# A pair table laid out by slot row, output products ahead of the last attention transposes, and a last tile summed on two engines

## The chip, the cores and the metric

The kernel runs on one core of one Trainium2 chip. The metric is the device time of one execution in microseconds (us). Besides its engines (TensorE or PE for matmuls, VectorE or DVE, ScalarE or ACT, GpSimd or POOL, SyncE or SP for queueing transfers) the core has 16 DMA engines, which all queues share.

## What is computed

One layer of an encoder over a prompt of 256 tokens and a sample of 512, in float32, model width 1024. Both sequences use the same weights and attend only within themselves.

```python
h = _rmsnorm(x, attn_norm[l])
proj = h @ w_in[l]
a = _mla(c_q, c_kv, k_pe, ...)              # 8 heads, latent attention
b = _diff_attention(dq, dk, dv, ...)        # 4 heads, (softmax1 - lam * softmax2) @ v, rmsnorm per head
x = x + jnp.concatenate([a, b], axis=-1) @ w_out[l]
x = x + _hier_moe(_rmsnorm(x, ffn_norm[l]), ...)
return _rmsnorm(x, final_norm)

# _hier_moe: the best of 4 groups, in it the best 2 of 8 experts
out = out + gates[:, e:e + 1] * ((silu(t @ w_gate[e]) * (t @ w_up[e])) @ w_down[e])
```

## The kernel before

The 768 tokens are 6 tiles of 128 (NT = 6; tiles 0 and 1 are the prompt). The order of each engine's work is written out by hand, engine by engine, and semaphores tie the engines together. An engine takes its instructions in that order, so one that waits holds back all that stand behind it. The stages:

**Attention.** 48 units (a head pair or a diff head, for one tile of queries) go through a pipeline on TensorE: score, `transpose_p` two steps later, `attend` three steps later. When the last unit of a batch of diff heads is through, ScalarE takes the outputs from the bank, GpSimd computes the norm of the batch (`od_norm`, L480 to L487) and scales it (`od_scale`, L729), TensorE transposes it (`transpose_o`, L1673), and VectorE copies it to `aT` (L1268). Behind the last unit `out_part(0, ...)` (L1690), the output projection of tile 0, is woven in. `out_part(t, part)` does the products `part` of the 16 of tile t (8 for each half of the columns; each is two matmuls in the trace).

**Output projection and routing.** For t = 1 to 5 TensorE does the 16 products of tile t, and among them, for tile t - 1, `x2_transpose` (L1721), `router` (L1732), whose result the semaphore `logits` tells to VectorE, and `rank` (L1745 to L1749), which counts with the masks of `route` which row of its expert's list a token gets. VectorE does for each tile: `residual` halves (L1283), copy of the transposes (L1289), `ffn_norm` (L1299), `route` (L1309 to L1328, a chain of small operations in which each waits for the last; L1323 and L1328 make the two masks), `place` and `slots` (L1361, L1365). TensorE waits for `ones_ready` ahead of tile 1's products: VectorE sets the ones (L1277) behind its last work on the attention.

**The pair table.** `pair_of_slot` in DRAM has 12 x 64 x 32 entries: block, slot row, expert. It is filled with a mark at the start (L536), GpSimd scatters the pair numbers of each tile into it (L745), two for each tile, the last two when all tiles are routed, and SyncE then loads all but block 0 of it twice, for the two halves of the partitions (L613). VectorE waits for both (`ids_further`, L1412 to L1414), between its work for expert 0 and that for expert 1. Block 0 comes from a product (`ids_main`) and needs no table.

**Experts.** TensorE runs each expert on up to 64 rows, and again for further blocks of a popular one: gate and up products (L1806, 32 matmuls), transposes of the next expert's rows (L1797), down products of the expert before (L1815), a transpose of h (L1845). ScalarE does silu (L1060), VectorE the product with up (L1436) and copies (L1441, L1457). Weights come through a ring of six slots.

**The end.** The two expert rows of each pair are loaded (L629, L631). For tiles 0, 2 and 4 VectorE adds them to the residual, times their gates (L1483, L1486); for tiles 1, 3 and 5 TensorE does it with diagonal matrices in two banks (L1915). `total_row(t)` is the sum in either place. ScalarE squares and takes the root (L1113, L1114), VectorE scales (L1491, L1493), SyncE stores. In VectorE's order: combine(4), final(2), final(3), final(4), final(5).

Two lines that the change turns on:

```python
ids_dram.rearrange("(b r e) o -> r b (e o)", b=NBLK, e=NE)      # L536, L614: 32 entries at a time
dve.scalar_tensor_tensor(slot_u[:, 2 * t:2 * t + 2], rank_f, float(NE), slot_f, ALU.mult, ALU.add)  # L1365
```

## Time and profile before

| | |
|---|---|
| median of 3 runs | 780.86 us (780.75 to 782.1) |
| profiled execution | 780.85 us |
| its span, first to last instruction | 779.1 us |
| mean granted TensorE clock | 0.987 |
| busy: TensorE / VectorE / ScalarE / GpSimd | 737.5 / 297.1 / 220.3 / 201.2 us |
| attention's last transposes | 375.3 us |
| output projection and routing | 359.7 to 480 us |
| experts | 481.5 to 747.3 us |
| last pair rows landed / last store issued | 769.7 / 776.9 us |

A row of a timeline has the start, the duration, the engine and line, the operation, what it writes and reads, how many instructions are merged, and in brackets the idle time of its engine before it and what ended that. The granted clock of TensorE is a share of its full 2.4 GHz; it has a second level of one half.

### The profile page before, as it was taken

To read this page: it belongs to the slowest core of one execution; us is meant where nothing else is said; L and a number is where in the kernel's file an instruction comes from. 1 tells how busy PE (TensorE), PEld (TensorE's weight loads), DVE (VectorE), ACT (ScalarE), POOL (GpSimd) and SP (SyncE) were. 2 spreads that over 40 slices of the span, in tenths; PEclk is the share of its full clock that TensorE was granted. 3 is DMA by queue.
4 is the path that set the end of the run, shared out by engine and by line. 5 is a ranking of instruction groups with operands and counts; after the bars stand their busy time and mean duration, and the time that the engine had idled before them with its cause. 6 is when DMAs were issued, how large, how long until landed. Compare 5 with 4: busy or idle time off the path is not lost.

```text
span 779.1 us, 12116 instructions
## 1 busy us (share of the span) xinstructions
PE 737.5 (95%) x3886; PEld 408.2 (52%) x3887; DVE 297.1 (38%) x812; ACT 220.3 (28%) x595; POOL 201.2 (26%) x474
## 2 busy tenths in 40 slices
PE   8999999999888999998999998899997999999995
PEld 4555554444355666665455565455553555555542
DVE  2442211010188989983445455112111121112127
ACT  3643211101176777663111121011111011111123
POOL 1232422220024220330201133253342434342110
PEclk9999999999999999999999998999999999999999
DMA  9703003000140000000598427999999779999748
GB/s 345 277 0 109 0 1 108 1 0 1 42 181 1 2 1 1 2 1 1 201 424 321 163 83 259 377 413 415 415 416 416 268 275 409 419 415 406 275 155 345
DMA packets 36887, 154.64 MB, mean 198 GB/s; under 512 B 9652, under 2 KB 10804, under 8 KB 23904
## 3 DMA queue, kind: packets, MB, share of 16 engines
q1 hardware_dynamic: 28112, 136.50, 44.6%
q0 software_dynamic: 7504, 15.23, 5.3%
q10 hardware_dynamic: 1216, 2.23, 0.8%
q8 instruction: 28, 0.46, 0.3%
q14 instruction: 27, 0.22, 0.1%
HBM read 142.29 MB, written 20.03 MB: 208 GB/s over the span
## 4 chain that ended last, share of the span: by engine, by line
PE 82%; DMA 7%; issue 3%; POOL 3%; DVE 2%; ACT 2%; SPq 1%; POOLq 0%; DVEq 0%; ACTq 0%
PE banks L1534 20%; PE banks L1806 17%; PE banks L1690 9%; PE banks L1815 9%; PE banks L1606 4%; PE banks L1641 4%; PE banks L1797 3%; PE banks L1660 2%; PE banks L1615 2%; PE banks L1557 2%; DMA arena<-pair_rows 2%; PE banks L1664 2%; DMA arena<-h_rows,arena 2%; PE banks L1570 1%; PE banks L1560 1%
## 5 line engine op out<-in xcount | busy, mean ns | idle before, releaser
L1534 PE MATMUL banks<-arena 128*128 128x512 f32 (+1 forms) x384 | 162.1, 575 | 2.0 <-issue 1.6
L1806 PE MATMUL banks<-arena 128*64 128x256 f32 x1280 | 148.8, 385 | 2.8 <-DVE arena L1457 0.9
L1806 PEld LDWEIGHTS banks<-arena 128*64 128x64 f32 x1280 | 93.6, 138 | 50.8 <-issue 6.6
L1534 PEld LDWEIGHTS banks<-arena 128*128 128x128 f32 x384 | 71.5, 191 | 78.3 <-issue 78.3
L1690 PE MATMUL banks<-arena 128*128 128x512 f32 x192 | 86.4, 598 | 1.1 <-DVE arena L1277 1.1
L1815 PE MATMUL banks<-arena 128*64 128x512 f32 x320 | 79.8, 610 | 1.2 <-ACT arena L1068 0.9
L1232 DVE TENSOR_REDUCE arena<-banks 128x1 f32<-128x512 f32 (+1 forms) x96 | 55.4, 599 | 48.8 <-PE banks L1606 42.0
L989 ACT ACTIVATE arena<-banks,arena 128x512 f32<-128x512 f32 (+1 forms) x96 | 58.4, 614 | 43.2 <-DVE arena L1235 22.2
L1436 DVE TENSOR_TENSOR arena<-arena,banks 128x128 f32<-128x128 f32 x40 | 11.6, 290 | 151.3 <-ACT arena L1060 151.2
L1690 PEld LDWEIGHTS banks<-arena 128*128 128x128 f32 x192 | 35.1, 190 | 38.8 <-issue 37.5
L1060 ACT ACTIVATE arena<-banks 128x128 f32<-128x128 f32 x40 | 11.2, 279 | 153.6 <-PE banks L1806 153.6
L769 POOL DMA_INDIRECT arena<-h_rows,arena x40 | 41.8, 1045 | 44.2 <-POOL arena L774 28.7
L918 ACT ACTIVATE arena<-banks,arena 128x512 f32<-128x512 f32 (+1 forms) x24 | 16.0, 667 | 104.7 <-PE banks L1534 104.7
L782 POOL DMA_INDIRECT pair_rows<-arena x36 | 36.4, 1012 | 31.5 <-POOL arena L780 31.5
L1641 PE MATMUL banks<-arena 128*128 128x128 f32 x240 | 36.2, 282 | 8.5 <-issue 5.2
L1641 PEld LDWEIGHTS banks<-arena 128*128 128x128 f32 x240 | 25.9, 141 | 31.0 <-issue 26.0
L1606 PE MATMUL banks<-arena 96*128 96x512 f32 (+1 forms) x96 | 40.0, 539 | 2.1 <-ACT arena L989 1.2
L480 POOL TENSOR_SCALAR arena<-arena 128x2 f32<-128x2 f32 (+1 forms) x8 | 1.6, 195 | 151.9 <-ACT arena L1017 151.9
L1068 ACT ACTIVATE arena<-banks 128x512 f32<-128x512 f32 x32 | 19.1, 597 | 70.1 <-PE banks L1815 70.1
L658 POOL TENSOR_TENSOR arena<-arena 128x64 f32<-128x64 f32 (+2 forms) x24 | 8.0, 333 | 115.9 <-ACT arena L918 67.5
L1815 PEld LDWEIGHTS banks<-arena 128*64 128x64 f32 x320 | 20.1, 137 | 27.4 <-issue 23.7
L1212 DVE COPY arena<-banks 128x512 f32<-128x512 f32 x12 | 8.3, 689 | 64.2 <-PE banks L1580 64.2
(204 smaller groups left out, 900.1 us busy)
## 6 DMA issues: line engine op xcount, KB each, us to landing
arena<-w_gate SPq DMA_DIRECT2D x32, 1024.0 KB, 11.3
arena<-w_up SPq DMA_DIRECT2D x32, 1024.0 KB, 11.1
arena<-w_down SPq DMA_DIRECT2D x32, 1024.0 KB, 11.2
arena<-w_in SPq DMA_DIRECT2D x3, 2048.0 KB, 8.2
arena<-pair_rows SPq DMA_DIRECT2D x5, 1024.0 KB, 11.2
arena<-w_out SPq DMA_DIRECT2D x1, 4096.0 KB, 13.0
arena<-x SPq DMA_DIRECT2D x6, 512.0 KB, 10.2
residual<-arena SPq DMA_DIRECT2D x6, 512.0 KB, 7.1
```

What stands on the lines that cost most here:

```text
L769: pool.indirect_dma_start(x_rows[i], None, h2_dram, bass.IndirectOffsetOnAxis(ap=rows, axis=0), bounds_check=2 * T - 1, oob_is_err=False). ...
L782: pool.indirect_dma_start(y_dram, bass.IndirectOffsetOnAxis(ap=yid_cur[:, i:i + 1], axis=0), y_sb[i], None, bounds_check=4 * T - 1, oob_is ...
L989: act.activation(p_tok[u % 3][:, a, 0:nt * P], bank(2 * (u % 2) + a)[:, 0:nt * P], ACT.Exp, bias=nbias[:, u % 4, a:a + 1], scale=MLA_SCALE ...
L1068: act.activation(y_sb[s % YBUF], bank(4), ACT.Copy).then_inc(y_out, 1)
L1232: dve.reduce_max(mx[:, u % 4, a:a + 1], bank(2 * (u % 2) + a)[:, 0:nt * P], X_).then_inc(dve_chain, 1)
L1534: last = nc.tensor.matmul(bank(mm % 2)[:, 0:GROUP_COLS[g]], xgT[:, t, c, :], w[:, c, :], start=(c == 0), stop=(c == DC - 1))
L1606: nc.tensor.matmul(bank(2 * (u % 2) + a)[:, 0:nt * P], qT[0:QK, 2 * j + a, tok], kT[0:QK, 2 * j + a, keys], start=True, stop=True).then_in ...
L1641: last = nc.tensor.transpose(bank(4 + tau % 2)[:, kt * P:(kt + 1) * P], p_tok[u % 3][:, a, kt * P:(kt + 1) * P], ident)
L1690: last = nc.tensor.matmul(bank(2 * (t % 2) + h), aT[:, t, c, :], w_out_sb[:, c, h * 512:(h + 1) * 512], start=(c == 0), stop=(c == DC - 1))
L1797: last = nc.tensor.transpose(bank(b)[:, c * P:(c + 1) * P], x_rows[i][:, c * P:(c + 1) * P], ident)
L1806: last = nc.tensor.matmul(bank(b)[h * SLOTS:(h + 1) * SLOTS, 0:2 * P].rearrange("p (g n) -> p g n", g=2), x_eT[i][:, 2 * (c % 4) + c // 4, ...
L1815: last = nc.tensor.matmul(bank(4)[h * SLOTS:(h + 1) * SLOTS, :], h_T[:, j * SLOTS:(j + 1) * SLOTS], w[:, j, h * 512:(h + 1) * 512], start= ...
```

## The change

It has three parts.

The pair table is laid out slot row first, then block, then expert: a pair of rank r with its expert e goes to (r mod 64) x 384 + (r div 64) x 32 + e, in place of r x 32 + e. The fill and the two loads then take each slot row in one piece. VectorE gets three operations more in `slots`.

On TensorE the first 8 products of tile 0 go ahead of `transpose_p` of the last unit (their wait for the exponentials is for the unit before it), four products of tile 1 go ahead of the last `transpose_o`, and the rest of tile 1's products is dealt out anew: 6, transposes, 3, router, rank, 3. Tiles 2 to 5 keep 3, transposes, 3, router, 7, rank, 3.

The last tile's sum is split: VectorE makes columns 0 to 511 (`combine_last`, ahead of final(4)), TensorE columns 512 to 1023. ScalarE squares the halves one by one, VectorE's first, and joins them through the bias of the root.

```diff
 
+        def total_half(t, h):
+
+            half = slice(h * 512, (h + 1) * 512)
+            return x_fin[:, t, half] if t == NT - 1 and h == 0 else total_row(t)[:, half]
+
         class Area:
...
         rank_f = m.take(2)
+        rank_u = m.take(2).bitcast(u32)
+        assert 1 << 6 == SLOTS
         onehot = m.take(2 * P).rearrange("p (i n) -> p i n", i=2)
...
             sp.wait_ge(consts_set, 2)
-            sp.dma_start(ids_dram.rearrange("(b r e) o -> r b (e o)", b=NBLK, e=NE),
-                         yids_sb[0:SLOTS, :].rearrange("r (b e) -> r b e", b=NBLK)).then_inc(ids_zeroed, 16)
+            sp.dma_start(ids_dram.rearrange("(r n) o -> r (n o)", r=SLOTS), yids_sb[0:SLOTS, :]).then_inc(ids_zeroed, 16)
             sp.wait_ge(odT_ready, 8)
...
             for h in range(2):
-                sp.dma_start(yids_sb[h * SLOTS:(h + 1) * SLOTS, NE:].rearrange("r (b e) -> r b e", e=NE),
-                             ids_dram.rearrange("(b r e) o -> r b (e o)", b=NBLK, e=NE)[:, 1:, :]).then_inc(ids_loaded, 16)
+                sp.dma_start(yids_sb[h * SLOTS:(h + 1) * SLOTS, NE:],
+                             ids_dram.rearrange("(r n) o -> r (n o)", r=SLOTS)[:, NE:]).then_inc(ids_loaded, 16)
             with sp.Fori(1, NGRP - 1) as g:
...
             act.wait_ge(act_chain, chain[0])
-            for t in range(NT):
+            for t in range(NT - 1):
                 if on_pe(t):
                     act.wait_ge(summed, t // 2 + 1)
                 else:
                     act.wait_ge(y_added, t // 2 + 1)
                 link(act.activation(junk_e, total_row(t), ACT.Square, accum_out=ss[:, t:t + 1]))
                 act.activation(rs[:, t:t + 1], ss[:, t:t + 1], ACT.Sqrt, bias=const("eps"), scale=1.0 / D).then_inc(rms_ready, 1)
+            for h, what, count in ((0, y_added, NT // 2 + 1), (1, summed, NT // 2)):
+                act.wait_ge(what, count)
+                link(act.activation(junk_e[:, h * 512:(h + 1) * 512], total_half(NT - 1, h), ACT.Square, accum_out=ss_c[:, h:h + 1]))
+                if h == 0:
+                    link(act.activation(ss_c[:, 0:1], ss_c[:, 0:1], ACT.Identity, bias=const("eps"), scale=1.0 / D))
+            act.activation(rs[:, NT - 1:NT], ss_c[:, 1:2], ACT.Sqrt, bias=ss_c[:, 0:1], scale=1.0 / D).then_inc(rms_ready, 1)
 
...
                 dve.wait_ge(dve_chain, chain[0])
-                dve.scalar_tensor_tensor(slot_u[:, 2 * t:2 * t + 2], rank_f, float(NE), slot_f, ALU.mult,
+                link(dve.tensor_copy(rank_u, rank_f))
+                link(dve.tensor_scalar(rank_u, rank_u, 6, None, ALU.logical_shift_right))
+                link(dve.scalar_tensor_tensor(slot_f, rank_u, float(NE - SLOTS * NBLK * NE), slot_f, ALU.mult, ALU.add))
+                dve.scalar_tensor_tensor(slot_u[:, 2 * t:2 * t + 2], rank_f, float(NBLK * NE), slot_f, ALU.mult,
                                          ALU.add).then_inc(slots_ready, 1)
...
                 link(dve.reciprocal(rs[:, t:t + 1], rs[:, t:t + 1]))
-                for half in ([slice(0, D)] if t < NT - 1 else [slice(0, 512), slice(512, D)]):
-                    dve.scalar_tensor_tensor(y_rows[:, 2 * t, half], total_row(t)[:, half], rs[:, t:t + 1], gain_fin[:, half],
+                if t < NT - 1:
+                    dve.scalar_tensor_tensor(y_rows[:, 2 * t, :], total_row(t), rs[:, t:t + 1], gain_fin,
                                              ALU.mult, ALU.mult).then_inc(final_ready, 1)
+                    return
+                for h in range(2):
+                    half = slice(h * 512, (h + 1) * 512)
+                    if h == 0:
+                        dve.wait_ge(summed, NT // 2)
+                    dve.scalar_tensor_tensor(y_rows[:, 2 * t, half], total_half(t, h), rs[:, t:t + 1], gain_fin[:, half],
+                                             ALU.mult, ALU.mult).then_inc(final_ready, 1)
+
+            def combine_last():
+
+                t = NT - 1
+                dve.wait_ge(yrows_in[t], 16)
+                x = x_fin[:, t, 0:512]
+                link(dve.scalar_tensor_tensor(x, y_rows[:, 2 * t, 0:512], gates[:, 2 * t:2 * t + 1], x, ALU.mult, ALU.add))
+                dve.scalar_tensor_tensor(x, y_rows[:, 2 * t + 1, 0:512], gates[:, 2 * t + 1:2 * t + 2], x, ALU.mult,
+                                         ALU.add).then_inc(y_added, 1)
 
...
                 final(t - 1 if t else 0)
+            combine_last()
             final(NT - 2)
...
                         pe.wait_ge(o_mla, len([u for u in range(N_UNITS) if is_mla(u) and UNITS[u][0] == 0]))
+                        pe.wait_ge(exps, 2 * N_UNITS - 2)
+                    if t == 1 and i == 0:
                         pe.wait_ge(exps, 2 * N_UNITS)
...
                     score(i)
+                if i == N_UNITS + 1:
+                    out_part(0, range(0, DC))
                 if 0 <= i - 2 < N_UNITS:
                     transpose_p(i - 2)
                 if 0 <= i - 3 < N_UNITS:
                     attend(i - 3)
                 u = i - O_LAG
-                if 0 <= u < N_UNITS and ends_batch(u):
+                if 0 <= u < N_UNITS - 1 and ends_batch(u):
                     transpose_o(u)
 
-                if i in (N_UNITS + 1, N_UNITS + 3):
-                    half = (i - N_UNITS) // 2
-                    out_part(0, range(half * DC, (half + 1) * DC))
+                if i == N_UNITS + 3:
+                    out_part(0, range(DC, 2 * DC))
 
...
 
+            out_part(1, range(0, 4))
+            transpose_o(N_UNITS - 1)
             pe.wait_ge(ones_ready, 1)
             for t in range(1, NT):
-                out_part(t, range(0, 3))
+                out_part(t, range(0, 3) if t > 1 else range(4, 10))
                 if t >= 2:
                     place(t - 2)
                 x2_transpose(t - 1, 0)
                 x2_transpose(t - 1, 1)
-                out_part(t, range(3, 6))
+                out_part(t, range(3, 6) if t > 1 else range(10, 13))
                 router(t - 1, 0)
                 router(t - 1, 1)
-                out_part(t, range(6, 13))
+                if t > 1:
+                    out_part(t, range(6, 13))
                 rank(t - 1)
...
                 last = None
-                for h in range(2):
+                for h in range(2) if t < NT - 1 else (1,):
                     half = slice(h * 512, (h + 1) * 512)
```

TensorE around the end of the attention, before. L1641 is `transpose_p`, L1660 and L1664 are `attend`, L1690 `out_part`, L1673 `transpose_o`, L1721 `x2_transpose`, L1732 `router`, L1747 the first product of `rank(0)`:

```order
L1641 MATMUL banks<-arena 128x128 x4
L1660 MATMUL banks<-arena 64x128 x8
L1690 MATMUL banks<-arena 128x512 x8
L1664 MATMUL banks<-arena 128x128 x4
L1690 MATMUL banks<-arena 128x512 x8
L1673 MATMUL banks<-arena 128x128 x4
L1690 MATMUL banks<-arena 128x512 x3
L1721 MATMUL banks<-arena 128x128 x8
L1690 MATMUL banks<-arena 128x512 x3
L1732 MATMUL banks<-arena 128x36 x8
L1690 MATMUL banks<-arena 128x512 x7
L1747 MATMUL banks<-arena 128x32
```

And now, with L1673 for `transpose_p`, L1692 and L1696 for `attend`, L1724 for `out_part`, L1705 for `transpose_o`, L1756, L1767, L1782 and L1784 for the transposes, the router and both products of the rank:

```order
L1724 MATMUL banks<-arena 128x512 x8
L1673 MATMUL banks<-arena 128x128 x4
L1692 MATMUL banks<-arena 64x128 x8
L1696 MATMUL banks<-arena 128x128 x4
L1724 MATMUL banks<-arena 128x512 x12
L1705 MATMUL banks<-arena 128x128 x4
L1724 MATMUL banks<-arena 128x512 x6
L1756 MATMUL banks<-arena 128x128 x8
L1724 MATMUL banks<-arena 128x512 x3
L1767 MATMUL banks<-arena 128x36 x8
L1782 MATMUL banks<-arena 128x32
L1784 MATMUL banks<-arena 128x32
```

The 8 products went ahead of the last `transpose_p`, four (the last of the 12) ahead of `transpose_o`, and the 7 that stood between router and rank of tile 0 are gone from there.

VectorE at the end of the program, before (scaling of tiles 2, 3, 4 and 5; L1491 is the reciprocal ahead of each):

```order
L1493 SCALAR_TENSOR_TENSOR arena<-arena 128x1024
L1491 RECIPROCAL arena<-arena 128x1
L1493 SCALAR_TENSOR_TENSOR arena<-banks,arena 128x1024
L1491 RECIPROCAL arena<-arena 128x1
L1493 SCALAR_TENSOR_TENSOR arena<-arena 128x1024
L1491 RECIPROCAL arena<-arena 128x1
L1493 SCALAR_TENSOR_TENSOR arena<-banks,arena 128x512 x2
```

And now, from the scaling of tile 3 on:

```order
L1506 RECIPROCAL arena<-arena 128x1
L1508 SCALAR_TENSOR_TENSOR arena<-banks,arena 128x1024
L1523 SCALAR_TENSOR_TENSOR arena<-arena 128x512
L1524 SCALAR_TENSOR_TENSOR arena<-arena 128x512
L1506 RECIPROCAL arena<-arena 128x1
L1508 SCALAR_TENSOR_TENSOR arena<-arena 128x1024
L1506 RECIPROCAL arena<-arena 128x1
L1515 SCALAR_TENSOR_TENSOR arena<-arena 128x512
L1515 SCALAR_TENSOR_TENSOR arena<-banks,arena 128x512
```

Two operations of 512 columns, the last tile's first half, stand between the scalings of tiles 3 and 4.

ScalarE at the end, before (square and root of tiles 4 and 5, behind the root of tile 3):

```order
L1114 ACTIVATE arena<-arena 128x1
L1113 ACTIVATE arena<-arena 128x1024
L1114 ACTIVATE arena<-arena 128x1
L1113 ACTIVATE arena<-banks 128x1024
L1114 ACTIVATE arena<-arena 128x1
```

And now (square and root of tile 4, then the last tile):

```order
L1119 ACTIVATE arena<-arena 128x1024
L1120 ACTIVATE arena<-arena 128x1
L1123 ACTIVATE arena<-arena 128x512
L1125 ACTIVATE arena<-arena 128x1
L1123 ACTIVATE arena<-banks 128x512
L1126 ACTIVATE arena<-arena 128x1
```

One square and one root of the last tile became square, scaled sum, square, root.

## Rows read from the trace of the kernel before

**Rows 1.** The chain that ended last, its share of the span by engine (page):

```profile
PE 82%; DMA 7%; issue 3%; POOL 3%; DVE 2%; ACT 2%; SPq 1%; POOLq 0%; DVEq 0%; ACTq 0%
```

**Rows 2.** Timeline of all engines from 340 to 396 us, TensorE's rows:

```profile
375.35 0.65 PE L1673 MATMUL banks<-arena 128*128 128x128 f32 x4 [0.74 <-POOL arena L729]
...
377.11 2.84 PE L1690 MATMUL banks<-arena 128*128 128x512 f32 x6 [1.10 <-DVE arena L1277]
```

**Rows 3.** The chain in order of time, 345 to 396 us: start, us, what:

```profile
385.11 6.09 PE banks L1690 x14
391.20 0.14 PE banks L1747 x2
```

**Rows 4.** Timeline of VectorE from 376 to 440 us:

```profile
385.15 0.26 DVE L1309 SCALAR_TENSOR_TENSOR arena<-banks,arena 128x36 f32<-128x36 f32 x1 [1.14 <-PE banks L1732]
...
387.31 0.24 DVE L1323 TENSOR_SCALAR arena<-arena 128x32 f32<-128x32 f32 x1
...
388.54 0.24 DVE L1328 TENSOR_SCALAR arena<-arena 128x32 f32<-128x32 f32 x1
...
392.69 0.16 DVE L1365 SCALAR_TENSOR_TENSOR arena<-arena 128x2 uint32<-128x2 f32 x1
394.33 0.69 DVE L1283 TENSOR_TENSOR arena<-arena,banks 128x512 f32<-128x512 f32 x1 [1.48 <-PE banks L1690]
```

**Rows 5.** Stretches (us, busy, PEclk, DMA share, GB/s), then TensorE's timeline:

```profile
496.00:500.00 4.00, 3.65 (x22) 0.62 1.05 408
...
606.00:608.00 2.00, 2.00 (x10) 0.50 0.58 234
...
496.35 4.97 PE L1806 MATMUL banks<-arena 128*64 128x256 f32 x32 [0.49 <-DVE arena L1457]
...
503.97 3.67 PE L1806 MATMUL banks<-arena 128*64 128x256 f32 x32
...
595.49 0.63 PE L1797 MATMUL banks<-arena 128*128 128x128 f32 x4 [2.63 <-DMA arena<-h_rows,arena]
...
604.38 0.67 PE L1797 MATMUL banks<-arena 128*128 128x128 f32 x4 [2.68 <-DMA arena<-h_rows,arena]
```

**Rows 6.** The table load: SyncE, landing, stretches, then timelines of VectorE and TensorE:

```profile
487.55 1.33 SPq L613 DMA_DIRECT2D arena<-pair_of_slot x2
...
DMA to landing us min/median/max: 3.9/4.8/5.7
...
490.00:491.00 1.00, 1.00 1.04 208
...
493.00:494.00 1.00, 1.00 1.02 418
...
493.89 0.34 DVE L1412 TENSOR_SCALAR arena<-arena 128x352 uint32<-128x352 uint32 x1 [7.18 <-DMA arena<-pair_of_slot]
...
495.13 0.29 DVE L1436 TENSOR_TENSOR arena<-arena,banks 128x128 f32<-128x128 f32 x1
...
490.85 1.94 PE L1815 MATMUL banks<-arena 128*64 128x512 f32 x8
495.47 0.39 PE L1845 MATMUL banks<-arena 128*128 128x128 f32 x1 [2.68 <-DVE arena L1436]
```

**Rows 7.** Timelines from 738 us on; the last two rows are ScalarE's at 465 us:

```profile
769.74 3.70 PE L1915 MATMUL banks<-arena 128*128 128x512 f32 x8 [1.76 <-DMA arena<-pair_rows]
...
772.26 1.28 DVE L1493 SCALAR_TENSOR_TENSOR arena<-arena 128x1024 f32<-128x1024 f32 x1
...
773.48 1.12 ACT arena L1113 x2
...
775.15 1.41 DVE L1493 SCALAR_TENSOR_TENSOR arena<-banks,arena 128x512 f32<-128x512 f32 x2
...
465.09 0.62 ACT L1024 ACTIVATE arena<-arena 128x512 bf16<-128x512 f32 x1
...
465.84 0.29 ACT L1030 ACTIVATE arena<-arena 128x1 f32<-128x1 f32 x1
```

## The prediction

> **What bounds the kernel now.** I read the chain of waits first: TensorE carries 82% of it [rows 1], so an edit counts where it moves TensorE or where TensorE stands still. Then I read the timelines of the three stretches that the edit touches, engine by engine. The reader is to see three things. (a) Behind the attention TensorE stands 0.74 us until GpSimd has scaled the last batch, and 1.10 us until VectorE has set the ones [rows 2]; after that it works without a gap through the routing stage, and VectorE's routing chains run beside products [rows 3, 4]. (b) At 492.8 us TensorE has nothing to do for 2.68 us, since VectorE waits for the pair table, and the products behind it run at the lower clock [rows 5, 6]. (c) Behind the last pair rows, TensorE, ScalarE and VectorE follow each other one at a time [rows 7]. The sum is made against the profiled execution: 780.85 us, of which 779.1 is its span; the median of the runs is 780.86, so the same sum serves both.
>
> **Part 1, the pair table by slot row.** Removed: each of the two loads of the table (L613) takes 64 x 11 pieces of 128 bytes; they become 64 pieces of 1408 bytes. The first load is issued at 487.55 and lands 3.9 us later, at 491.5; the second lands at 493.87, where VectorE goes on, 5.7 us behind an issue at 488.2 [rows 6]. So the second comes in 2.4 us behind the first though it was issued 0.65 behind it, and while they run the queues move 208 GB/s instead of the 418 just behind them [rows 6]: the small pieces cost time of their own. With an eleventh of the pieces both should land between where the first landed (491.5) and a point not long after their issue. What follows the landing on VectorE: three operations on the table, from 493.89 to 495.13, 1.24 us, then the product of silu and up (0.29, L1436). TensorE's down products end at 490.85 + 1.94 = 492.79 [rows 6]. It is not held at all if the h product ends by then: landing at or before 492.79 - 0.29 - 1.24 = 491.26. I take that (the upper end, 491.5, is only 0.24 later), so the 2.68 us of idle time go, and with them the short wait for VectorE's copy behind it. Only the transpose of h (L1845, 0.33) stands between the down products and the next gate and up products, so the group that starts at 496.35 starts near 493.1: 3.25 us earlier. That group also took 4.97 us against 3.67 for the same 32 matmuls one expert later, since the granted clock was 0.62 in 496 to 500 [rows 5]; without the gap it should be at full clock: 1.3 us more. Part 1 gains 3.25 + 1.3 = 4.55, say 4.6; bounds: 0 (landing set by the weight loads ahead of it in the queue alone) to 4.7. I take 4.6, since 208 GB/s is a row on exactly these pieces.
>
> The Trainium skill ("DMA: Bandwidth & Descriptors", section "Anatomy of one DMA", written for GpSimd's path) speaks against this part: a transfer costs a fixed 2 us, mostly the receipt of the last write, plus its bytes, and many descriptors can be issued before their number shows. By it the two loads of 88 KB cost about 2.2 us in either layout, the rest of 5.7 us is queueing behind the weights, and part 1 gains next to nothing; the row of 208 GB/s disagrees.
>
> Added to part 1: three chained VectorE operations of two columns in each of the six slots steps. The nearest row is L1365, 0.16 us, and with the hand-over 0.2, so 0.6 us per tile. For five tiles the next thing on VectorE is the second residual half, which stood 1.48 us waiting for TensorE [rows 4]: covered, and 0.6 us dearer each if that cover were gone. For the last tile the scatter is issued from GpSimd several us later than the slots are there. The clearing store at the start is one issue long ahead of its use. These cost nothing. Scatter addresses change, their number and size do not: nothing.
>
> **Part 2, output products ahead of the last transposes.** Moved first: the 8 products of tile 0, first half, go from behind the last unit's transposes and the products of the unit before it to ahead of them. TensorE had no gap between those, and the last attend came behind all of it anyway; its transposed input is copied by VectorE beside the other unit's attend. Nothing gained, and nothing lost as long as that copy is no longer than that attend. Moved second: four products of tile 1 go ahead of the transposes of the last batch (L1673). They cover the 0.74 us wait for GpSimd [rows 2]: -0.7. The wait for the ones (1.10) stays where it was, right behind these transposes, because VectorE sets them only after it has read the transposes: 0. Who waits behind: SyncE's loads of gain, bias and weights start with VectorE's copy of these transposes, now some 2.7 us later; of these tile 0's norm needs the gain and the bias, and that norm too moves back, by the same and by three products more, so it is covered. The weights are wanted a whole stage later.
>
> Moved third, and dearest: tile 1 had 7 products between router(0) and rank(0). They took 6.09 us of the stretch from 385.11 [rows 3] and hid VectorE's route(0). In the new order all of tile 1's products but the last three are spent before the router, and the rank products stand directly behind it. They need the masks of L1323 and L1328. Those are made from 385.15 on and are there at 387.31 + 0.24 = 387.55 and at 388.54 + 0.24 = 388.78 [rows 4]. So TensorE has to stand from router end for 3.7 us (385.11 to 388.82), less the 0.14 us of the first two rank matmuls: 3.55. A restart behind a gap costs some 0.25 more (six matmuls took 2.84 behind the gap at 377.11, where 14 in a row took 6.09, 0.435 each: 2.61) [rows 2, 3]. Part 2 in work and idle time: -0.7 + 3.55 + 0.25 = +3.1. Nothing hides it: the chain runs through TensorE from here to the end of routing.
>
> Then the clock. TensorE stood 2.68 us before 495.5 and before 604.4, and both times it worked at the lower of its levels behind it (0.62 over four us; the products behind the first took 4.97 instead of 3.67) [rows 5]. It stood 2.63 us before 595.5, and did not fall. The new gap is 3.7 us with two matmuls of 32 columns in it, longer than all of these. I take the fall: 1.3 to 1.4 us, the price paid at 496. Part 2: +4.5; bounds 2.9 (no fall) to 5.0.
>
> **Part 3, the last tile's sum.** The rows land at 769.7. Before, TensorE makes both halves in 3.70 us from 769.74, ScalarE squares 1024 columns from 773.48 (1.12) and takes the root (0.3 as in L1030), VectorE scales twice (775.15 on) [rows 7]. Now VectorE makes the first half, but it is busy with tiles 2 and 3 until 772.1 (its scaling of tile 4 starts at 772.26, behind a reciprocal). Two operations on 512 columns at 0.7 each, the half of 1.41 for two of that size: done at 773.5, just when TensorE used to be done. ScalarE then does, one behind the other: square of 512 columns (0.75, from 465.09 to 465.84), the scaled half sum (0.3, L1030), square of the other half (0.75), root (0.3): 2.1 instead of 1.42 [rows 7]. TensorE's half is ready at 771.6 and waits. So the last reciprocal comes 0.65 us later. Tile 4's own output also goes behind by 1.45 us and shares the queues with the last two halves: 0 to 0.3. Part 3: +0.8; bounds 0.6 to 1.2; it loses unless ScalarE took the finished half first, and the order written takes the late one first.
>
> **The sum.** -4.6 + 4.5 + 0.8 = +0.7; with 780.86 that is 781.6. I say 781.5.
>
> **Rivals.**
> 1. The table load gains next to nothing, because the weight loads ahead of it on the same queue set its landing. VectorE still waits until about 493.5, the gap and the low clock stay. (This is also what comes out by the Trainium skill's page above.) For: the queues are full, 418 GB/s behind it. Against: the 2.4 us between two landings [rows 6]. It ends on the slower side: -0.4 + 4.5 + 0.8 = +4.9, 785.8; a half measure (landing at 492.5, TensorE held 1.2 us) would be 783. It decides if the landing is after 492.8. Chance 0.15.
> 2. The clock holds through the new gap, because the two rank matmuls stand in it. For: the gap before 595.5. Against: the gaps before 495.5 and 604.4, both shorter. 781.5 - 1.4 = 780.1. Chance 0.18.
> 3. The clock falls at some other gap that it now survives: the gap before 595.5 is as long as the two that fell, and both parts shift where the gaps lie. +1.4: 782.9. Chance 0.14.
> 4. The stall behind router(0) isn't there, because the masks come sooner than TensorE (route(0) hidden by something I don't see): -4.6 - 0.7 + 0.8 = -4.5, 776.4. Against: the order of both engines is written out, and each step of route(0) waits for the one before. Chance 0.10, with smaller gains elsewhere that I miss.
> 5. My forecast: 0.43.
>
> **Numbers.** A measurement of this kernel tells 0.2% (1.6 us) from no change: the bounds are 779.3 and 782.4. The forecast and rival 2 lie inside, rivals 1 and 3 mostly above, rival 4 below. Faster 0.12, same 0.55, slower 0.33. The range reaches to rival 3 and the half measure of rival 1 above, and to rival 2 with part 3 at its lower end below: 778.9 to 784.3.
>
> **What would show it.** Part 1: the gap of VectorE before its first table operation falls from 7.18 us to under 4.5, TensorE has no gap near 493, and the group of 32 matmuls there takes 3.7 instead of 5.0. Part 2: no wait for GpSimd before the transposes of the last batch, and a wait of about 2.4 and one of 1.1 us before the first and the second pair of rank matmuls of tile 0, with a granted clock under 1 behind them. Part 3: ScalarE's square of the last tile starts with VectorE's half at about 0 to 0.1 us after the time at which TensorE's both halves were done, measured from the landing of the last rows, and the last scaling ends 0.7 us later than before on that scale. The prediction is wrong if the table lands after the down products end, or if rank(0) doesn't wait.

## The result and the profile after

| | before | changed |
|---|---|---|
| median, 8 runs each on one chip | 781.97 us (780.75 to 784.84) | 787.4 us (785.18 to 789.3) |
| profiled execution | 780.85 us | 787.19 us |
| its span | 779.1 us | 785.3 us |
| mean granted TensorE clock | 0.987 | 0.977 |

The change costs 0.70% (95% interval of the ratio 1.0047 to 1.0093), 5.4 us by the medians. 781.5 us had been forecast, with a range of 778.9 to 784.3, so the result lies above the range, and near rival 1 (785.8, +4.9).

I cut the two profiled spans at marks that both programs have: the start of the last attention matmuls, TensorE's first product of `place(0)`, its first gate product and the end of the experts' last gate and up products (the last down products and the summing stand behind that mark). "Low" is the time lost to the lower clock in that stage, worked out from the granted clock of windows of 1 us: TensorE's busy time in each, times what the clock lacks to 1.

| stage | before, us (low) | changed, us (low) | difference |
|---|---|---|---|
| up to the last attention matmuls | 356.4 (1.7) | 358.4 (4.8) | +2.0 |
| to `place(0)`: the moved products, `router(0)`, `rank(0)` | 40.3 (0.0) | 45.8 (3.0) | +5.5 |
| to the first gate product | 84.9 (3.4) | 84.9 (3.2) | 0.0 |
| experts, to the last gate and up products | 261.3 (3.2) | 259.1 (3.4) | -2.2 |
| from there to the end | 36.3 (0.0) | 37.1 (0.0) | +0.8 |

The chain of waits reads as before [rows 1], TensorE carries it (shares by engine in the changed kernel's page):

```profile
PE 83%; DMA 7%; DVE 3%; issue 3%; POOL 2%; ACT 1%; SPq 0%; POOLq 0%; ACTq 0%; DVEq 0%
```

The first row of the table isn't the change's work: both programs do the same there, but the clock stood lower. These are windows of before (first) and of the changed kernel (stretch, its length, busy time of TensorE, of its weight loads, VectorE, ScalarE and GpSimd, then PEclk, DMA share, GB/s). They lose 0.06 x 26.3 = 1.6 us and 0.17 x 27.2 = 4.6 us. In the profiles of this study that place loses anything from 0 to 5.1 us, with the same TensorE instructions in all of them:

```profile
200.00:230.00 30.00, 26.27 (x119) 14.56 (x117) 15.56 (x53) 14.17 (x53) 1.93 (x10) 0.94 0.39 144
```

```profile
200.00:230.00 30.00, 27.23 (x108) 15.65 (x107) 13.23 (x45) 11.97 (x44) 0.39 (x3) 0.83 0.37 144
```

The other rows are the three parts. **Part 2** first: TensorE's timeline of the changed kernel (start, duration, line, what was merged, idle time ahead), beside which [rows 2, 3] stand for before, then its windows:

```profile
379.90 0.60 PE L1705 MATMUL banks<-arena 128*128 128x128 f32 x4
381.60 5.42 PE L1724 MATMUL banks<-arena 128*128 128x512 f32 x12 [1.10 <-DVE arena L1289]
...
390.31 1.87 PE L1767 MATMUL banks<-arena 128*128 128x36 f32 x16
394.76 0.61 PE L1782 MATMUL banks<-arena 128*128 128x32 f32 x2 [2.58 <-DVE arena L1335]
395.90 0.63 PE L1784 MATMUL banks<-arena 128*128 128x32 f32 x2 [0.53 <-DVE arena L1340]
```

```profile
392.00:396.00 4.00, 0.89 (x5) 0.67 (x4) 3.26 (x16) 0.00 (x0) 0.00 (x0) 0.83 1.01 404
396.00:400.00 4.00, 4.00 (x7) 1.93 (x8) 2.92 (x20) 0.72 (x2) 0.00 (x0) 0.50 1.01 425
400.00:404.00 4.00, 4.00 (x9) 1.72 (x8) 0.69 (x1) 1.31 (x4) 0.00 (x0) 0.81 1.02 426
```

The wait for GpSimd ahead of `transpose_o` (L1705) is gone, the one for the ones (1.10) is the same as in [rows 2], and `rank(0)` stands for its two masks, 2.58 and 0.53 us. Just ahead of the first of its matmuls the clock falls, and it comes back only behind 401 us: 0.17 x 4 + 0.5 x 4 + 0.19 x 4 = 3.4 us of clock, of which 3.0 while TensorE worked.

The kernel before has such a place itself, and I had overlooked it: `rank(5)`, the last one, with four products between router and rank instead of seven, waits for the same two masks (L1747 and L1749 are `rank`'s products with them). TensorE's timeline of before, then its windows:

```profile
470.34 0.41 PE L1747 MATMUL banks<-arena 128*128 128x32 f32 x2 [0.95 <-DVE arena L1323]
471.57 0.53 PE L1749 MATMUL banks<-arena 128*128 128x32 f32 x2 [0.82 <-DVE arena L1328]
```

```profile
472.00:476.00 4.00, 4.00 (x14) 2.97 (x14) 2.43 (x18) 0.00 (x0) 0.00 (x0) 0.50 0.74 300
476.00:480.00 4.00, 3.97 (x8) 1.35 (x6) 1.63 (x8) 0.00 (x0) 2.56 (x3) 0.68 0.16 43
```

Behind two waits of under 1 us the clock is low from 471 to 479 us and TensorE loses 3.3 us of work. That is the row nearest to the new stall, on the same instructions, and its price is what the new stall cost. It isn't the same in every profile: behind the same two waits t_first_old and t_first_new (below) hold the upper level.

**Part 1**: the table load in the changed kernel. SyncE's timeline first, to be read beside [rows 6]:

```profile
487.00 1.29 SPq L554 DMA_DIRECT2D arena<-w_down  x3
494.92 1.13 SPq L619 DMA_DIRECT2D arena<-pair_of_slot  x2
497.10 0.35 SPq L554 DMA_DIRECT2D arena<-w_gate  x1
```

The answer on line 619, and the windows (stretch, length, PEclk, DMA share, GB/s):

```profile
DMA to landing us min/median/max: 3.2/4.1/5.0
```

```profile
497.00:498.00 1.00, 1.00 0.68 213
498.00:499.00 1.00, 1.00 0.95 223
```

VectorE's and then TensorE's timeline:

```profile
500.48 0.34 DVE L1427 TENSOR_SCALAR arena<-arena 128x352 uint32<-128x352 uint32 x1 [6.21 <-DMA arena<-pair_of_slot]
```

```profile
498.41 1.94 PE L1853 MATMUL banks<-arena 128*64 128x512 f32 x8
502.08 0.33 PE L1883 MATMUL banks<-arena 128*128 128x128 f32 x1 [1.73 <-DVE arena L1451]
502.97 5.36 PE L1844 MATMUL banks<-arena 128*64 128x256 f32 x32 [0.57 <-DVE arena L1472]
```

With an eleventh of the pieces the second load still takes 1.8 us longer from issue to landing than the first (5.0 against 3.2; before 5.7 against 3.9). The stretch at 213 GB/s is there too, though the DMA engines were less busy in it (share 0.68, against 1.04 in [rows 6]). The down products end at 500.35, the table is used from 500.48, TensorE stands 1.73 us, and the 32 matmuls behind it take 5.36 us at the lower clock.

The -2.2 us of the experts' stage is only in part this gap, 0.95 us less than before. The rest is a wait for gathered rows, `h_rows`, the one of 2.68 us before 604.4 in [rows 5]: in the changed kernel it is 1.21 us. That wait varies from under 0.6 to 2.72 us over the kernels of this study, in ones that leave the table alone too (0.85 in c_last, 2.72 in b_first8), so nothing here lays it on the layout.

**Part 3**: the end of the changed kernel, ScalarE and VectorE in one timeline (beside [rows 7]):

```profile
775.29 1.98 PE L1953 MATMUL banks<-arena 128*128 128x512 f32 x4 [1.91 <-DMA arena<-pair_rows]
...
778.22 0.75 DVE L1524 SCALAR_TENSOR_TENSOR arena<-arena 128x512 f32<-128x512 f32 x1
...
779.01 0.63 ACT L1123 ACTIVATE arena<-arena 128x512 bf16<-128x512 f32 x1 [2.76 <-DVE arena L1524]
...
780.09 0.60 ACT L1123 ACTIVATE arena<-banks 128x512 bf16<-128x512 f32 x1
...
780.81 0.29 ACT L1126 ACTIVATE arena<-arena 128x1 f32<-128x1 f32 x1
781.14 0.16 DVE L1506 RECIPROCAL arena<-arena 128x1 f32<-128x1 f32 x1 [0.77 <-ACT arena L1126]
```

From the landing of the last rows to the last reciprocal: 781.14 - 775.29 = 5.85 us; before, with the reciprocal 0.2 ahead of the scaling, it was 775.15 - 0.2 - 769.74 = 5.2. ScalarE stands 2.76 us for VectorE's half, with TensorE's half ready at 777.3.

### The profile page after: what moved, and what is told of

It is laid out like the page before. It is cut to its first block, busy times and chain, and to the rows that moved or that the text cites. A ratio compares the mean times of both kernels' runs of the same rounds, so it can differ in the third digit from the quotient of the medians.

```text
span 785.3 us, 12129 instructions
## 1 busy us (share of the span) xinstructions
PE 740.0 (94%) x3880; PEld 411.1 (52%) x3881; DVE 301.1 (38%) x832; ACT 221.0 (28%) x598; POOL 201.1 (26%) x474
## 4 chain that ended last, share of the span: by engine, by line
PE 83%; DMA 7%; DVE 3%; issue 3%; POOL 2%; ACT 1%; SPq 0%; POOLq 0%; ACTq 0%; DVEq 0%
PE banks L1566 20%; PE banks L1844 17%; PE banks L1724 11%; PE banks L1853 9%; PE banks L1638 5%; PE banks L1673 4%; PE banks L1835 3%; PE banks L1647 2%; PE banks L1692 2%; PE banks L1696 2%; PE banks L1589 2%; DMA arena<-h_rows,arena 2%; DMA arena<-pair_rows 2%; PE banks L1602 1%; PE banks L1592 1%
## 5 line engine op out<-in xcount | busy, mean ns | idle before, releaser
L1724 PE MATMUL banks<-arena 128*128 128x512 f32 x192 | 88.6, 611 | 1.1 <-DVE arena L1289 1.1
L1724 PEld LDWEIGHTS banks<-arena 128*128 128x128 f32 x192 | 36.1, 196 | 40.7 <-issue 39.4
L1673 PE MATMUL banks<-arena 128*128 128x128 f32 x240 | 36.8, 285 | 8.1 <-issue 5.7
L1638 PE MATMUL banks<-arena 96*128 96x512 f32 (+1 forms) x96 | 41.9, 562 | 2.1 <-ACT arena L995 1.2
L1673 PEld LDWEIGHTS banks<-arena 128*128 128x128 f32 x240 | 26.7, 143 | 31.1 <-issue 26.6
L1853 PEld LDWEIGHTS banks<-arena 128*64 128x64 f32 x320 | 20.2, 137 | 27.2 <-issue 23.6
```

Of the source, the lines that this page charges most:

```text
L1638: nc.tensor.matmul(bank(2 * (u % 2) + a)[:, 0:nt * P], qT[0:QK, 2 * j + a, tok], kT[0:QK, 2 * j + a, keys], start=True, stop=True).then_in ...
L1673: last = nc.tensor.transpose(bank(4 + tau % 2)[:, kt * P:(kt + 1) * P], p_tok[u % 3][:, a, kt * P:(kt + 1) * P], ident)
L1724: last = nc.tensor.matmul(bank(2 * (t % 2) + h), aT[:, t, c, :], w_out_sb[:, c, h * 512:(h + 1) * 512], start=(c == 0), stop=(c == DC - 1))
L1853: last = nc.tensor.matmul(bank(4)[h * SLOTS:(h + 1) * SLOTS, :], h_T[:, j * SLOTS:(j + 1) * SLOTS], w[:, j, h * 512:(h + 1) * 512], start= ...
```

## The experiments

All are compared with the kernel before on the same chip (6 to 12 runs of each kernel, 23 to 35 of before beside them). A difference in us behind "measured" is the ratio times the median of before, so it can stand some tenths off the difference of the two medians. "Stage" is the stage to `place(0)` in the profile, before 40.3 us. Only one of them changes what is computed: `b_spare` makes four products more that nobody reads.

| kernel | median, us | before, us | ratio (95%) | stage (low), us | mean clock of all runs |
|---|---|---|---|---|---|
| changed | 787.4 | 781.97 | 1.0070 (1.0047 to 1.0093) | 45.8 (3.0) | 0.979 |
| a_table | 781.01 | 782.28 | 0.9981 (0.9957 to 1.0006) | 41.9 (1.7) | 0.986 |
| b_products | 788.99 | 782.28 | 1.0077 (1.0055 to 1.0100) | 47.9 (5.0) | 0.981 |
| c_last | 782.07 | 781.85 | 1.0010 (0.9988 to 1.0033) | 40.3 (0.0) | 0.983 |
| t_first_old | 779.36 | 782.28 | 0.9956 (0.9936 to 0.9975) | 40.2 (0.0) | 0.987 |
| t_first_new | 778.67 | 782.28 | 0.9951 (0.9924 to 0.9977) | 40.2 (0.0) | 0.989 |
| b_spare | 783.72 | 781.85 | 1.0023 (0.9998 to 1.0049) | 43.0 (0.0) | 0.986 |
| b_covered | 785.31 | 781.85 | 1.0039 (1.0013 to 1.0065) | 44.1 (3.4) | 0.982 |
| b_first8 | 782.41 | 782.16 | 0.9999 (0.9977 to 1.0020) | 42.0 (1.7) | 0.986 |
| b_one | 782.8 | 782.16 | 1.0001 (0.9981 to 1.0021) | 39.4 (0.0) | 0.984 |
| c_swapped | 781.83 | 781.85 | 1.0005 (0.9983 to 1.0026) | 40.2 (0.0) | 0.985 |
| best_old | 776.17 | 782.16 | 0.9927 (0.9905 to 0.9948) | 39.4 (0.0) | 0.990 |
| all_mended | 776.34 | 782.16 | 0.9931 (0.9911 to 0.9950) | 41.0 (1.7) | 0.985 |

The kernel before has a mean clock of 0.986 over the 82 runs taken beside these.

### Each part alone

**a_table** is part 1 alone:

```diff
-                sp.dma_start(yids_sb[h * SLOTS:(h + 1) * SLOTS, NE:].rearrange("r (b e) -> r b e", e=NE),
-                             ids_dram.rearrange("(b r e) o -> r b (e o)", b=NBLK, e=NE)[:, 1:, :]).then_inc(ids_loaded, 16)
+                sp.dma_start(yids_sb[h * SLOTS:(h + 1) * SLOTS, NE:],
+                             ids_dram.rearrange("(r n) o -> r (n o)", r=SLOTS)[:, NE:]).then_inc(ids_loaded, 16)
...
+                link(dve.tensor_copy(rank_u, rank_f))
+                link(dve.tensor_scalar(rank_u, rank_u, 6, None, ALU.logical_shift_right))
+                link(dve.scalar_tensor_tensor(slot_f, rank_u, float(NE - SLOTS * NBLK * NE), slot_f, ALU.mult, ALU.add))
```

> The kernel before with part 1 of the change alone (table by slot row, three more VectorE operations per tile). Pieces theory (my prediction): the small pieces of the two table loads were what kept VectorE, so it goes on at least 2.5 us earlier, the gap of 2.68 us on TensorE before the h transpose of expert 1 closes and the time falls by 3 to 4.6 us. Queue theory (from the trace of the changed kernel): the landing is set by the three down-weight loads issued some 8 us ahead on the same queue; the load lands 0.5 to 1 us earlier, VectorE's wait is about 6.2 instead of 7.18, TensorE keeps a gap of about 1.7 us, and the time falls by 0 to 1.5 us. VectorE's added operations cost nothing under either.

Measured: 0.9981, an interval that holds 1. VectorE waits 6.51 us for the table, the landings are 3.1 to 4.8 us behind the issues, and TensorE stands 2.02 us. So part 1 gives some 1.5 us, perhaps nothing, and not 4.6.

**b_products** is part 2 alone:

```diff
+                if i == N_UNITS + 1:
+                    out_part(0, range(0, DC))
...
+            out_part(1, range(0, 4))
+            transpose_o(N_UNITS - 1)
...
-                out_part(t, range(0, 3))
+                out_part(t, range(0, 3) if t > 1 else range(4, 10))
...
-                out_part(t, range(3, 6))
+                out_part(t, range(3, 6) if t > 1 else range(10, 13))
...
-                out_part(t, range(6, 13))
+                if t > 1:
+                    out_part(t, range(6, 13))
```

> The kernel before with part 2 alone (output products ahead of the last transposes). TensorE loses the 0.74 us wait before the last batch's transposes and gets a wait of 2.6 and one of 0.5 to 1.1 us before the two pairs of rank matmuls of tile 0. Stall alone: +3.1 us. Stall and one spell at the lower clock (3.4 us long): +4.5. Stall and two such spells, as in the profile of the changed kernel: +5.5.

Measured: 1.0077, +6.0 us: the whole loss of the changed kernel and a little more. `rank(0)` stands 2.58 and 0.76 us. The stage is 7.6 us longer, of which 5.0 is the lower clock. But of these 5.0 us only 3.2 lie behind the stall (from 397 to 404 us). The other 1.7 are a stretch from 359 to 364 us, ahead of the router, which a_table, b_first8 and all_mended have in their profiles too and before hasn't: scatter, like that of the first stage.

**c_last** is part 3 alone (the part's lines of the diff ahead of the prediction, unchanged):

```diff
+            for h, what, count in ((0, y_added, NT // 2 + 1), (1, summed, NT // 2)):
+                act.wait_ge(what, count)
...
+            combine_last()
             final(NT - 2)
...
-                for h in range(2):
+                for h in range(2) if t < NT - 1 else (1,):
```

> Part 3 alone (last tile's sum shared). By the sum of the prediction: +0.65 to +0.8 us, since ScalarE does square, scaled sum, square, root behind VectorE's half. Under the rival that the shared sum helps, -0.5 us.

Measured: 1.0010, +0.8 us, which alone the interval doesn't tell from nothing; but in the profile the stretch from the experts' last gate and up products to the end is 37.1 us, as in the changed kernel, against 36.3. This stretch is steady: from the end of the last down products on it is 31.8 to 32.0 us in the seven profiles that have the old last tile and no work at the lower clock there, and 32.6 in both with the shared one.

The three ratios multiplied give 0.9981 x 1.0077 x 1.0010 = 1.0068, and the changed kernel has 1.0070: the parts add up, and within the intervals there is no fourth cause to look for.

### What sets the landing of the table

Rival 1 says that the weight loads ahead in the queue do. **t_first_old** keeps the old layout with its 128-byte pieces and issues the two small loads ahead of the three loads of `w_down` on SyncE (the wait for the first gathered rows goes with it; the wait for the scatters, now ahead of all five loads, stands in its place):

```diff
-            sp.wait_ge(rows_in[0], 16)
-            for slot in (4, 5):
-                load_part(2, 0, slot)
-            residual_free(NT)
-            load_part(2, *LAST)
             sp.wait_ge(ids_scattered, 2 * NT * 16)
             for h in range(2):
                 sp.dma_start(yids_sb[h * SLOTS:(h + 1) * SLOTS, NE:].rearrange("r (b e) -> r b e", e=NE),
                              ids_dram.rearrange("(b r e) o -> r b (e o)", b=NBLK, e=NE)[:, 1:, :]).then_inc(ids_loaded, 16)
+            for slot in (4, 5):
+                load_part(2, 0, slot)
+            residual_free(NT)
+            load_part(2, *LAST)
```

> The kernel before, its table layout untouched (64 x 11 pieces of 128 bytes), with the two table loads issued ahead of the three down-weight loads (experts 4, 5 and the last) instead of behind them. Queue theory: with nothing large ahead the second load lands 2 to 3 us behind its issue (5.7 before) even with the small pieces; VectorE's wait falls from 7.18 to about 4 us, TensorE's gap closes, the matmuls behind it run at the full clock, and the time falls by 3 to 4.6 us. Pieces theory: the load still takes about 4 us or more, and the gap closes by half at most: -1 to -2 us. The down weights come some 8 us later; if they are then late, TensorE waits at the down products of expert 4 or 5.

Its timeline of SyncE, and the answer on line 608:

```profile
486.65 1.32 SPq L608 DMA_DIRECT2D arena<-pair_of_slot  x2
488.02 1.60 SPq L548 DMA_DIRECT2D arena<-w_down  x3
```

```profile
DMA to landing us min/median/max: 2.5/2.6/2.7
```

VectorE's and then TensorE's timeline:

```profile
490.25 0.33 DVE L1411 TENSOR_SCALAR arena<-arena 128x352 uint32<-128x352 uint32 x1
```

```profile
482.03 0.65 PE L1796 MATMUL banks<-arena 128*128 128x128 f32 x4 [2.78 <-DMA arena<-h_rows,arena]
483.56 5.26 PE L1805 MATMUL banks<-arena 128*64 128x256 f32 x32 [0.88 <-DVE arena L1467]
...
494.48 1.94 PE L1814 MATMUL banks<-arena 128*64 128x512 f32 x8
496.35 0.33 PE L1844 MATMUL banks<-arena 128*128 128x128 f32 x1
496.61 3.67 PE L1805 MATMUL banks<-arena 128*64 128x256 f32 x32
```

The same small pieces land in 2.5 to 2.7 us, nobody waits for them, TensorE has no gap near 494, and its 32 matmuls there take 3.67 us: all that part 1 was meant to bring, with the old layout. Counted from `place(0)`, at 398.72 here and 396.63 before, this group starts 1.8 us earlier, and it is 1.3 shorter, together 3.1. Measured: 0.9956, 3.4 us. The two rows at 482 show that the profile isn't free of gaps: a wait of 2.78 us for gathered rows that before doesn't have, with the lower clock behind it. It ends before the table loads are issued (486.65), so it isn't these loads that hold TensorE there. It is 2.04 us in t_first_new, 1.15 in best_old, 1.11 in b_products and under 0.6 in all_mended; what sets it stays open.

**t_first_new** is the same with the new layout (a_table's edit and the order above):

```diff
+                sp.dma_start(yids_sb[h * SLOTS:(h + 1) * SLOTS, NE:],
+                             ids_dram.rearrange("(r n) o -> r (n o)", r=SLOTS)[:, NE:]).then_inc(ids_loaded, 16)
+            for slot in (4, 5):
+                load_part(2, 0, slot)
```

> The same early issue of the table loads, with the table by slot row (part 1). Queue theory: the same time as with the old layout within 0.5 us, since the gap is closed already; the landing is shorter by what the pieces cost, 0.5 to 1 us. Pieces theory: at least 1.5 us faster than the old layout with the same issue.

Measured: 0.9951, with landings of 2.3 to 2.5 us. Ahead of the weights the layout is worth 0.2 us of flight and nothing that can be measured in the time (the intervals of the two lie over one another); the place in the queue is worth up to 3.0 us of flight (5.7 against 2.7). Over the kernels of this study that leave the loads behind the weights and keep the old layout, VectorE's wait was 5.45 to 7.18 us and TensorE's gap 0.94 to 2.68; before's, which I priced, is the longest of the eight. The two with the new layout, 6.21 and 6.51 us of wait and gaps of 1.73 and 2.02, lie inside these ranges, and so does their slower landing (5.0 and 4.8 us, where the eight have 3.8 to 5.7): behind the weights the profiles don't tell the layouts apart.

### Stall and clock behind the router

**b_spare** is part 2, with TensorE kept busy while VectorE makes the masks:

```diff
-                out_part(t, range(6, 13))
+                if t > 1:
+                    out_part(t, range(6, 13))
+                else:
+                    for i in range(4):
+                        nc.tensor.matmul(bank(5), aT[:, 1, 0, :], w_out_sb[:, 0, 0:512], start=True, stop=True)
```

> Part 2 alone, with four extra products of 512 columns (3.44 us, results unused) between router(0) and rank(0), which TensorE does while it would wait for the masks. It tells the clock from the stall: if the lower clock costs 1.4 to 2.4 us of part 2, this is faster than part 2 alone by that much and ends some 3.1 us above the kernel before with a granted clock of 1.0 in the stretch; if the stall alone makes the loss, it is as slow as part 2 alone.

TensorE's timeline, and the window over its end:

```profile
388.38 1.87 PE L1735 MATMUL banks<-arena 128*128 128x36 f32 x16
390.09 3.68 PE L1785 MATMUL banks<-arena 128*128 128x512 f32 x8
393.60 0.30 PE L1750 MATMUL banks<-arena 128*128 128x32 f32 x2
```

```profile
392.00:396.00 4.00, 3.93 (x13) 1.93 (x12) 3.65 (x20) 0.72 (x2) 0.00 (x0) 1.00 1.02 427
```

The unused work fills the stall, even a little more than that: `rank(0)` starts 5.2 us behind the router's start, where it was 4.45 in b_products. But the clock stays at its upper level, and the stage is 43.0 us, +2.7, against +7.6 in b_products. Measured: 1.0023, +1.8 us, where b_products had +6.0. So of part 2's loss some 2 to 2.7 us are idle time, and the rest goes with the lower clock: the time of the runs gives it 4.2 us (the two intervals don't overlap), the profile 3.2 behind the stall.

**b_covered** is part 2 with the seven products dealt so that six of them stand between router and rank again:

```diff
-                out_part(t, range(0, 3))
+                out_part(t, range(0, 3) if t > 1 else range(4, 6))
...
-                out_part(t, range(3, 6))
+                out_part(t, range(3, 6) if t > 1 else range(6, 7))
...
-                out_part(t, range(6, 13))
+                out_part(t, range(6, 13) if t > 1 else range(7, 13))
```

> Part 2 alone, but tile 1's remaining products dealt out as 2, transposes, 1, router, 6, rank, 3, so that six products (5.2 us) cover route(0) again. If the loss of part 2 is the uncovered routing chain, no wait stands before rank(0), the granted clock stays at 1.0 there, and the time is that of the kernel before or up to 0.7 us under it (four products cover GpSimd's scaling; a short wait for the residual halves may take some of it back). If the loss lies in the move of tile 0's first eight products, it stays at 3 us or more.

TensorE's timeline, then its windows:

```profile
383.70 1.98 PE L1692 MATMUL banks<-arena 128*128 128x512 f32 x4 [1.10 <-DVE arena L1277]
385.53 1.04 PE L1724 MATMUL banks<-arena 128*128 128x128 f32 x8
386.40 1.02 PE L1692 MATMUL banks<-arena 128*128 128x512 f32 x2
388.62 2.56 PE L1735 MATMUL banks<-arena 128*128 128x36 f32 x16 [1.19 <-ACT arena L1038]
390.98 5.47 PE L1692 MATMUL banks<-arena 128*128 128x512 f32 x6
```

```profile
388.00:392.00 4.00, 3.38 (x18) 2.87 (x19) 2.13 (x6) 0.56 (x2) 0.69 (x1) 0.73 0.99 411
392.00:396.00 4.00, 4.00 (x6) 1.66 (x5) 3.55 (x16) 0.17 (x1) 0.10 (x1) 0.50 1.00 420
```

Measured: 1.0039, +3.1 us. This one went against me. The stall ahead of `rank(0)` is gone, but with one product left between the transposes and the router TensorE waits 1.19 us for ScalarE ahead of the router, 5 us behind the 1.10 for the ones, and the clock falls there all the same: the stage is 44.1 us, 3.4 of it clock. In this profile the clock falls behind two waits of just over 1 us among short matmuls, which I had thought only a long gap brings. How regularly it does is open: the mean clock of the runs is lower too (0.982), but so is c_last's (0.983), where TensorE does the same as before up to the end.

**b_first8** moves only the first 8 products of tile 0:

```diff
+                if i == N_UNITS + 1:
+                    out_part(0, range(0, DC))
...
-                if i in (N_UNITS + 1, N_UNITS + 3):
-                    half = (i - N_UNITS) // 2
-                    out_part(0, range(half * DC, (half + 1) * DC))
+                if i == N_UNITS + 3:
+                    out_part(0, range(DC, 2 * DC))
```

> The kernel before with only the first move of part 2: tile 0's first eight products ahead of the last unit's transposes and of the attend before it. Under my account this costs and gains nothing: the stretch from the last transposes of attention probabilities to the first id product stays at 40.3 us. If the loss of part 2 lay in it, the stretch is 1 us or more longer, with the last batch's scaling on GpSimd later.

Measured: 0.9999. This move is free, as it had been priced; its stage is 1.7 us longer by a stretch at the lower clock near 360 us, of which the time of the runs shows nothing; it is the same stretch as in b_products and a_table.

**b_one** puts only one product of tile 1 ahead of the last `transpose_o` and leaves the seven behind the router:

```diff
+            out_part(1, range(0, 1))
+            transpose_o(N_UNITS - 1)
...
-                out_part(t, range(0, 3))
+                out_part(t, range(0 if t > 1 else 1, 3))
```

> The kernel before with one product of tile 1 (0.86 us) ahead of the last batch's transposes, in place of four, and the rest of its order as before: 2, transposes, 3, router, 7, rank, 3. It covers GpSimd's 0.74 us without uncovering route(0): the stretch from the last transposes of attention probabilities to the first id product takes 39.6 to 39.8 us instead of 40.3, no low clock in it, and the time falls by 0.5 to 0.7 us, which a measurement may not tell from none. If the transposes' late place itself costs (VectorE, then the ones, then TensorE), the stretch stays at 40.3 or more.

TensorE's timeline:

```profile
376.93 0.66 PE L1673 MATMUL banks<-arena 128*128 128x128 f32 x4
378.69 1.98 PE L1692 MATMUL banks<-arena 128*128 128x512 f32 x4 [1.11 <-DVE arena L1277]
```

One product (two instructions of 0.435, 0.87 us) covers the wait for GpSimd, and the stage is 0.9 us shorter. Measured: 1.0001: in the time that gain isn't seen. (Its runs have a lower mean clock than before, 0.984 against 0.986, which may hide it.)

### The last tile

**c_swapped** is part 3 with ScalarE taking TensorE's half, the one that is ready first:

```diff
-            for h, what, count in ((0, y_added, NT // 2 + 1), (1, summed, NT // 2)):
+            for h, what, count in ((1, summed, NT // 2), (0, y_added, NT // 2 + 1)):
```

> Part 3 alone, but ScalarE takes TensorE's half first (it is ready some 2 us earlier) and VectorE's second. If the loss is the order on ScalarE, the last root comes 1.0 us earlier than in part 3 alone, so 0.2 to 0.4 us under the kernel before; if VectorE's two operations ahead of tile 4's scaling or the stores set the end, nothing changes against part 3 alone.

The timeline of ScalarE and VectorE:

```profile
772.04 0.60 ACT L1122 ACTIVATE arena<-banks 128x512 bf16<-128x512 f32 x1 [0.91 <-PE banks L1943]
...
773.94 0.63 ACT L1122 ACTIVATE arena<-arena 128x512 bf16<-128x512 f32 x1 [0.89 <-DVE arena L1520]
773.96 1.28 DVE L1504 SCALAR_TENSOR_TENSOR arena<-arena 128x1024 f32<-128x1024 f32 x1
...
774.70 0.29 ACT L1125 ACTIVATE arena<-arena 128x1 f32<-128x1 f32 x1
...
775.16 0.15 DVE L1502 RECIPROCAL arena<-arena 128x1 f32<-128x1 f32 x1
```

The end stage is 36.6 us, 0.5 less than c_last and still 0.3 more than before (0.1 to 0.3 more than the seven profiles with the old last tile). What is late now isn't ScalarE (its root is done at 775.0) but VectorE, which scales tile 4 for 1.28 us just when the root comes. The time doesn't tell it from before (1.0005).

### A version that beats both

**best_old** is the kernel before with the table loads first and b_one's single product:

```diff
             sp.wait_ge(ids_scattered, 2 * NT * 16)
...
+            for slot in (4, 5):
+                load_part(2, 0, slot)
...
+            out_part(1, range(0, 1))
+            transpose_o(N_UNITS - 1)
```

> The kernel before, old table layout, with the table loads ahead of the down weights and with the one product of tile 1 ahead of the last transposes: by the two single effects -3.4 and -0.6, so -4.0 us, 0.995 of the kernel before.

Measured: 0.9927 (0.9905 to 0.9948), 776.17 us: 6.0 us faster than before and 11 faster than the changed kernel. **all_mended** has the same two edits with the new layout and c_swapped's last tile:

```diff
-            out_part(1, range(0, 4))
+            out_part(1, range(0, 1))
             transpose_o(N_UNITS - 1)
...
-            for h, what, count in ((0, y_added, NT // 2 + 1), (1, summed, NT // 2)):
+            for h, what, count in ((1, summed, NT // 2), (0, y_added, NT // 2 + 1)):
```

> The changed kernel with its three parts mended: new table layout with its loads ahead of the down weights, one product instead of four ahead of the last transposes with route(0) covered, last tile shared with ScalarE taking TensorE's half first. Expected -3.8 (table) -0.6 (products) +0.0 to -0.3 (last tile): about -4.5 us, 0.994 of the kernel before. If the layout adds something of its own it is more than 0.5 us faster than the version with the old layout; I expect no such difference.

Measured: 0.9931, the same within the intervals. The layout and the split sum bring nothing on top. Both gain more than their parts did alone (0.9956 x 1.0001 = 0.9957); best_old has a higher mean clock than before (0.990 against 0.986), but all_mended hasn't (0.985), so the clock doesn't explain both, and what does stays open. In their profiles the `h_rows` wait near 600 us is 0.97 and 0.90 us, where before and t_first_old have 2.68: 1.7 us less. But it varies without any of these edits, as said above, and one profile each doesn't make it the cause.

### How much of the time is the clock

One profile shows one course of the clock, but each run comes with its mean clock and its span. Over all 211 runs, with a level of its own for each kernel and session, a run whose mean clock is 0.001 lower takes 0.45 us longer (standard error 0.03); what is left scatters by 1.25 us, where the 82 runs of before reach from 777.9 to 787.9. By a profile, 1.7 us lost at half the clock is 3.4 us low, which lowers the mean by 0.5 x 3.4 / 780 = 0.0022: 0.78 us per 0.001. The two differ, perhaps because low stretches fall in part on idle time (not shown), so I take both as ends:

| | time over before, us | mean clock under before | of it clock, us | rest, us |
|---|---|---|---|---|
| changed | +5.2 | 0.0071 | 3.2 to 5.5 | -0.3 to 2.0 |
| b_products | +6.6 | 0.0054 | 2.4 to 4.2 | 2.4 to 4.2 |
| b_covered | +3.3 | 0.0041 | 1.8 to 3.2 | 0.1 to 1.5 |
| b_spare | +1.7 | 0.0001 | 0.1 | 1.6 |
| c_last | +0.1 | 0.0034 | 1.5 to 2.6 | -2.6 to -1.4 |

(Means over all runs here, against the mean of before in the same session; for the changed kernel, of the 82.) By this account more than half of what the change costs is the clock. The last row shows how far it can be off: c_last touches nothing but the end, its profile is 0.8 us longer there, and the account gives it a gain of 1.4 to 2.6 us beside a lower clock that nothing in its edit explains. So it is good to some 2 to 3 us, enough for the first two rows and not for b_covered.

## Why the prediction was wrong, and where it was right

**Part 1 is the step that failed.** The sum had -4.6 for it, "since 208 GB/s is a row on exactly these pieces"; a_table measured -1.5 (-3.4 to +0.5). Two readings were wrong. The 208 GB/s in [rows 6] isn't the pieces' price: the changed kernel, with an eleventh of the pieces, has 213 and 223 GB/s at the same place. It is a stretch where the weight loads issued earlier have run dry and the next `w_gate` has only just been issued (497.10 there), behind two loads that carry little. (The order of the issues says so; no run takes it apart. The small pieces do keep the DMA engines busier in it, a share of 1.04 against 0.68, but the landing hardly moved.) And the 2.4 us between the two landings isn't either: it is 2.3 us with large pieces (0.5 between the issues, 1.8 of flight) and 0.8 (0.6 and 0.2) with small pieces and no weights ahead. Rival 1 had this mechanism, its price and the condition ("if the landing is after 492.8", when the down products end): in the changed kernel the table is used 0.13 us behind the end of the down products. It got a chance of 0.15, because I let one row decide against it that has two readings; a look at which loads were under way in that window would have shown it. The Trainium skill ("DMA: Bandwidth & Descriptors", section "Anatomy of one DMA"), whose 2 us are given for GpSimd's path, came near here too: a fixed time near 2 us, and many descriptors before their number shows. SyncE's two loads took 2.3 to 2.7 us without weights ahead, 0.2 of it for eleven times as many pieces. The same page, section "Two DMAs through the same engine are not ordered", says that descriptors of one queue of a DMA engine start in order; t_first_old agrees, with landings 1.4 and 3.0 us sooner behind the issue from another place in the queue.

**The single row of 2.68 us.** TensorE's gap that part 1 was to remove came out at 0.94 to 2.68 us over the eight profiles with the loads behind the weights. I took the longest for the value. Had the landing been as I thought, 3 us would have been nearer than 4.6, and t_first_old with no gap at all gives 3.4 (2.0 to 5.0).

**Part 2, idle time: right, a little high.** +3.1 had been worked out: -0.7 for the wait for GpSimd (gone, as forecast), +3.55 of standing behind the router (2.58 + 0.53 = 3.1 measured; the masks took 3.6 us as in [rows 4], and the second pair of rank matmuls started 3.7 us behind the router as forecast, but the first pair, at the lower clock, filled 0.6 us of that and not 0.14), +0.25. The stage without its clock is 45.8 - 3.0 - 40.3 = +2.5, and b_spare's +2.7. The two waits named ("about 2.4 and one of 1.1 us") were 2.58 and 0.53. Rival 4 (no stall) is out.

**Part 2, clock: the term was mis-sized.** That it falls was right and rival 2 wrong. It had been priced at 1.4 with [rows 5] as the only measure, and measured 3.0 in the changed kernel and 3.2 in b_products behind the stall: the clock stays low for 6.9 us there (windows from 392 to 404), not for the 3.4 us of the place from which I took the price. The row to take was that of `rank(5)` at 470 us, where the kernel before stands for the same masks and loses 3.3 us. The prediction says that behind the attention TensorE works without a gap through the routing stage; these two waits of 0.95 and 0.82 us are what it missed. With 3.3 in place of 1.4 part 2 comes to +6.4, where b_products measured +6.0. With the bounds of 2.9 to 5.0 for all of part 2, the +6.0 (4.3 to 7.8) of b_products is above the upper end. Rival 3, the clock falling elsewhere too, came true in the profile, at 200 to 230 us, in a stretch that the change doesn't touch, so as scatter and not as its effect.

**Part 3: right.** +0.8 forecast, +0.8 in both profiles; ScalarE's four steps took 781.10 - 779.01 = 2.09 us where 2.1 had been worked out. That taking the finished half first would save it was half right: it saves 0.5 of the 0.8.

**What was costed at nothing cost nothing.** The three operations in `slots` took 0.17, 0.17 and 0.16 us, and the stage to the first gate product is 84.9 us in both. The first eight products moved: 0.9999.

The sum with the measured terms: -1.5 + 6.0 + 0.8 = +5.3, against +5.4. The forecast of "same" hung on two large terms of opposite signs, each with one row behind it, and the range wasn't as wide as their bounds: part 1 at 0 and part 2 at its upper end make 780.9 + 5.0 + 0.8 = 786.7, which the range left out, and 787.4 lies above even that. That the sum of the measured terms fits to 0.1 us is luck, with intervals of 1.8 to 2 us on either side of each.

## What to carry to other kernels

- The small load that VectorE waits for was late by what was ahead of it in its queue, hardly by its pieces: issue such a load ahead of the bulk loads before changing its layout.
- Products that hide a chain on another engine are the dearest to move. Spending them earlier to close a gap of 0.7 us opened one of 3.1, and the clock behind it cost 3.0 to 3.2 more; b_one closed the same 0.7 with one product and left the cover where it was.
- A price is taken from the row nearest in kind. The wait at the last `rank` was in the trace of before, with the same instructions and the same masks, and had the clock's price in it; the gap at 493 us was another sort of place.
- A row of low bandwidth needs its second reading: what was queued at that time. And where a gain and a loss of several us are added, the range is that of their bounds together.

## What the runs showed of the hardware

- The clock behind a stall can stay low for much longer than the stall: 3.1 us of standing, 6.9 us low; in the kernel before, waits of 0.95 and 0.82 us around two short matmuls, 6.8 us low (behind the same two waits it held in t_first_old and t_first_new). With the stall behind the router filled by products that nobody reads, it didn't fall there, and the kernel was 4 us faster than without them (1.0023 against 1.0077).
- It also fell in b_covered behind waits of 1.10 and 1.19 us, 5 us apart among transposes and router matmuls, while in before it held through 0.74 and 1.10 us [rows 2]. The Trainium skill ("TensorE: Matmul & The Clock Gate", section "A second HAM failure mode: psum-queue depth-cycling") tells of another kernel, in bf16, in which short and frequent idle times between groups of matmuls make the clock swing. This row is of that kind, but it is one fall in one profile. Removing a long gap by making two short ones is no sure cure.
- The run-to-run scatter of this kernel goes with the clock: 0.45 us for each 0.001 of the mean. Runs of one and the same kernel have mean clocks of 0.976 to 0.993 and times of 777.9 to 787.9 us, so one profile's low stretches (0 to 6.7 us up to the last attention matmuls, where TensorE does the same in all the kernels here) are a draw and not the kernel's price, and a difference of under 2 us between two profiles says little before it is seen stage by stage.
